# Sample attention: scores of old and appended keys in one hi/lo product, and a value product that runs ahead

## The reference

```
c_kv, k_rope = past latents and rotary keys (512 rows a stream) + 16 new rows
kvb    = c_kv @ w_kv_b                     # per head 64 for keys, 64 for values
k_nope = rmsnorm(kvb[..., :64], k_norm)    # a norm per key row and head
s = (q_nope . k_nope + q_rope . k_rope) * ATTN_SCALE
p = softmax(s);  o = p @ v;  mix = o @ w_o
```

## Time and profile before

| | us |
|---|---|
| median of 3 runs (lowest, highest) | 1978.94 (1974.6, 1982.67) |
| the profiled execution's own time | 1974.86 |
| its span in the profile | 1973.1 |
| TensorE busy (matmul) in the span | 1901.7 |
| VectorE / ScalarE / POOL busy | 1136.4 / 819.5 / 235.3 |
| sample attention, 1487.5 to 1600.0 | 112.5 |

### The profile page before, as it was taken

One profiled execution on the slowest core, in us unless ns is written; L12 is line 12 of the kernel. 1 busy time (PEld: TensorE's weight loads), 2 busy tenths in 40 slices (PEclk: granted clock), 3 DMA queues, 4 the chain that ended last, 5 costly groups with the idle time before them and its releaser, 6 DMA issues.

```text
span 1973.1 us, 28535 instructions
## 1 busy us (share of the span) xinstructions
PE 1901.7 (96%) x10641; PEld 1773.1 (90%) x10641; DVE 1136.4 (58%) x1800; ACT 819.5 (42%) x1428; POOL 235.3 (12%) x338
## 2 busy tenths in 40 slices
PE   9999998999998999999999999989999999999997
PEld 9999998788887999999999999876767779999997
DVE  6555448778779655445855544465654545555444
ACT  5333335555463433334533333355443324333233
POOL 1000110220210000011400002140012222000020
PEclk9999998999999999999999999899999999999999
DMA  5344444455342534444344444430022213444441
GB/s 198 126 128 128 139 148 141 135 176 203 111 181 91 174 125 126 130 136 129 115 140 128 128 135 132 166 101 22 33 66 79 80 51 119 125 124 126 136 138 64
DMA packets 63413, 243.33 MB, mean 123 GB/s; under 512 B 7681, under 2 KB 7761, under 8 KB 62049
## 3 DMA queue, kind: packets, MB, share of 16 engines
q1 hardware_dynamic: 54000, 196.67, 31.7%
q0 software_dynamic: 9328, 45.51, 6.6%
HBM read 230.32 MB, written 11.83 MB: 123 GB/s over the span
## 4 chain that ended last, share of the span: by engine, by line
PE 86%; DVE 7%; ACT 4%; issue 2%; POOL 0%; DMA 0%; SPq 0%; ACTq 0%; DVEq 0%; POOLq 0%
PE bank L1647 23%; PE bank L1649 23%; PE bank L1648 23%; PE bank L2155 2%; PE bank L2112 1%; PE bank L2057 1%; DVE wlo L1054 1%; PE bank L1844 1%; ACT seg L756 1%; PE bank L2059 1%; ACT kn L964 1%; PE bank L2058 1%; PE bank L1654 1%; PE bank L1655 1%; PE bank L1656 1%
## 5 line engine op out<-in xcount | busy, mean ns | idle before, releaser
L1647 PE MATMUL bank<-xh,whi 128*128 128x384 f32 x1960 | 665.7, 340 | 15.1 <-DVE xl L1064 13.2
L1649 PE MATMUL bank<-xh,wlo 128*128 128x384 f32 x1960 | 658.8, 336 | 0.0
L1648 PE MATMUL bank<-xl,whi 128*128 128x384 f32 x1960 | 658.8, 336 | 0.0
L1054 DVE TENSOR_TENSOR wlo<-raw,whi 128x1024 fp32r<-128x1024 f32 (+3 forms) x372 | 463.8, 1248 | 177.8 <-ACT whi L627 169.3
L627 ACT ACTIVATE whi<-raw 128x1024 fp32r<-128x1024 f32 (+2 forms) x369 | 378.9, 1029 | 296.4 <-PE bank L1649 282.4
L1647 PEld LDWEIGHTS bank<-xh,whi 128*128 128x128 f32 x1960 | 371.1, 189 | 25.3 <-issue 14.8
L1648 PEld LDWEIGHTS bank<-xl,whi 128*128 128x128 f32 x1960 | 371.2, 189 | 1.8 <-issue 1.2
L1649 PEld LDWEIGHTS bank<-xh,wlo 128*128 128x128 f32 x1960 | 370.5, 189 | 0.0
L1647 PE MATMUL bank<-ah,whi 128*128 128x384 f32 x704 | 237.2, 337 | 3.5 <-DVE tu L1075 3.3
L1074 DVE TENSOR_TENSOR tg<-bank,rstd 128x384 f32<-128x384 f32 x88 | 49.1, 557 | 331.1 <-PE bank L1649 330.5
L1649 PE MATMUL bank<-ah,wlo 128*128 128x384 f32 x704 | 236.8, 336 | 0.0
(11 more groups left out here) (379 smaller groups left out, 2280.7 us busy)
## 6 DMA issues: line engine op xcount, KB each, us to landing
raw<-in_stream SPq DMA_DIRECT2D x372, 512.0 KB, 3.6
S<-in_ssm POOLq DMA_DIRECT2D x4, 2048.0 KB, 9.1
out_ssm_s<-S POOLq DMA_DIRECT2D x4, 2048.0 KB, 8.0
cTb<-in_cacheT POOLq DMA_DIRECT2D x16, 512.0 KB, 3.8
seg<-acs_rows POOLq DMA_DIRECT2D x12, 512.0 KB, 5.1
lowC<-in_cache POOLq DMA_DIRECT2D x8, 512.0 KB, 3.8
h<-in_x SPq DMA_DIRECT2D x2, 768.0 KB, 5.9
lowA<-in_wkT POOLq DMA_DIRECT2D x4, 384.0 KB, 5.5
```

What stands on the lines that cost most here:

```text
L1054: V.tensor_tensor(wlo[:, r, 0:w], raw[:, r, 0:w], whi[:, r, 0:w].bitcast(F32), ALU.subtract).then_inc(lo_ready, 1)
L1647: M(out, whi[:, r, ws], mh_(k), start=first and k == k0, stop=False)
L1648: M(out, whi[:, r, ws], ml_(k), start=False, stop=False)
L1649: ins = M(out, wlo[:, r, ws], mh_(k), start=False, stop=last and k == k1 - 1)
```

## The change

- The 16 new keys of a stream are appended to its 512 past ones: `cTh`, `cTl` and `cTb` have 528 columns (`KEYS`). The latent query is split too: `QCh` and `QCl`, which live in the slots of `whi` and `wlo`. A unit's scores (`s_scores`) are 12 fp32r matmuls of 264 columns into two banks (`pair[1]`), and 2 for the rotary part into `pair[2]`. For the latter, high, low and high rows of 32 stand on each other (`q_stack`, `k_stack`, 96 rows). The rotary queries are stacked into `xh` and `xl` during the prompt heads.
- Each stream's latent is loaded once more and split once more for that (`keys_split`, on ScalarE and VectorE). From stream 2 on it comes into one buffer `craw`, and the rotary keys of every stream into one buffer `kraw`.
- The key factors are transposed once (`rs_turn`), stored to DRAM (`rs_rows`), and loaded for each unit with every row repeated 16 times (`past_rstd_rows` into `kn`). POOL's copies, the four transposes of a unit and the copy L1007 go.
- The maximum and the exponential go over 528 columns at once. The probabilities are scaled by the reciprocal of their sum before they are transposed, where the output was scaled after.
- The value product is turned: latent rows stationary, the probabilities of both units of a stream (`PTs`, 256 columns) moving, so that the output comes out turned. `s_values(n)` does half c of the 256 features of stream b, `b, c = divmod(n, 2)`; each half is issued two units after its unit. `s_turn`, L1622 and L1608 go; ScalarE copies the result (`s_latent`).
- Since `QCh` and `QCl` use the weight slots, the first three blocks of the output projection are split behind the loop. The reciprocals of `ksq` are taken in parts, streams 0 to 5 in the last prompt heads, 6 and 7 after.

The diff, cut to its core:

```diff
 # POOL
+            pool.wait_ge(rs_ev, 2)
+            pool.dma_start(rs_past(0, 6, 0, 3 * P), rsT[0:6 * MH, :]).then_inc(rs_st, 16)
+            pool.dma_start(rs_past(0, 6, 3 * P, P), rsT2[0:6 * MH, 0:P]).then_inc(rs_st, 16)
             for x in range(0, MH, MH // 4):
                 pool.wait_ge(qk_ps, x + MH // 4)
                 pool.dma_start(wkT[0:QD, x:x + MH // 4], T["wkT"][:, x:x + MH // 4]).then_inc(wkT_ld, 16)
+            def past_keys(b):
...
+                    pool.wait_ge(qc_ps, 8)
+                    pool.wait_ge(past_lo, STREAMS + b)
+                    pool.dma_start(craw, T["cacheT"][b]).then_inc(c_ld[b % 2], 16)
+            def past_rope(b):
...
+                    pool.wait_ge(stack_lo, 2 + b)
...
+                pool.dma_start(kraw[:, 0:PAST], T["krcT"][b]).then_inc(rope_ld, 16)
+                pool.dma_start(kraw[:, PAST:KEYS], kr_spread(b)).then_inc(rope_ld, 16)
+            def past_values(b):
+                pool.wait_ge(po_ps, MH + 2 * max(b - 1, 0))
                 pool.dma_start(cnat[:, b % 2], T["cache"][b]).then_inc(cn_ld[b % 2], 16)
+                pool.dma_start(vnew[0:STEPS, b % 2, :], ckv[STEPS * b:STEPS * b + STEPS, 2, :]).then_inc(cn_ld[b % 2], 16)
+            def past_rstd_rows(u):
+                if u >= 2:
+                    pool.wait_ge(s_added, u - 1)
+                pool.dma_start(kn[:, u % 2, 0:KEYS], rs_spread(u)).then_inc(rk_ld[u % 2], 16)
...
+            for u in range(2, UNITS):
+                b = u // 2 + 1
+                if u % 2 == 0 and b < STREAMS:
+                    past_keys(b)
+                    past_rope(b)
...
+                past_rstd_rows(u)
+                if u % 2 and b < STREAMS:
+                    past_values(b)
 # ScalarE
+            for u in range(UNITS):
+                if u >= 2:
+                    s_latent(u - 2)
+                if u + 1 < UNITS:
+                    s_exp(u + 1)
+                s_turned(u)
+                if u % 2 == 0 and 2 <= u // 2 + 2 < STREAMS:
+                    keys_split(u // 2 + 2)
 # VectorE
+            s_max(0)
+            keys_split(1)
             for u in range(UNITS):
                 dve.wait_ge(s_exp_ready, u + 1)
+                step(V.reciprocal(sm[:, o + 5:o + 6], sm[:, o + 4:o + 5]))
+                V.tensor_scalar(Pb[:, s, 0:KEYS], Pb[:, s, 0:KEYS], sm[:, o + 5:o + 6], None, ALU.mult).then_inc(p_ready, 1)
                 if u + 1 < UNITS:
                     s_max(u + 1)
+                if u % 2 == 0 and 2 <= u // 2 + 2 < STREAMS:
+                    keys_split(u // 2 + 2)
 # TensorE
+            for u in range(UNITS):
+                if u >= 2:
+                    s_values(u - 2)
+                if u + 1 < UNITS:
+                    s_scores(u + 1)
+                pe.wait_ge(p_ready, MH + u + 1)
+                pe.wait_ge(pt_ev, MH + u)
                 for j in range(5):
                     ins = nc.tensor.transpose(bank[6][:, tiles(j)] if j < 4 else bank[0][:, 0:P], Pb[:, u % 2, tiles(j)], ident[:, :])
                 ins.then_inc(pt_ps, 1)
```

More of the change, by code:

```diff
@@ L111, in build @@
         rows = sb("rows", [P, 2, TT])
-        bank = [ctx.enter_context(nc.psum_tensor(f"bank{i}", [P, 512], F32)) for i in range(8)]
+        pair = [ctx.enter_context(nc.psum_tensor(f"pair{i}", [P, 2, 512], F32)) for i in range(4)]
+        bank = [pair[i // 2][:, i % 2, :] for i in range(8)]
         with ExitStack() as ffn:
@@ L327, in build @@
         qc_ps = sem("qc_ps")
+        qc_hi = sem("qc_hi")
         qc_ev = sem("qc_ev")
[L329 to L334, removed]
+        stack_hi = sem("stack_hi")
+        stack_lo = sem("stack_lo")
+        rs_turn_ps = sem("rs_turn_ps")
+        rs_ev = sem("rs_ev")
+        rs_st = sem("rs_st")
+        rk_ld = [sem(f"rk_ld{i}") for i in range(2)]
         s_added = sem("s_added")
@@ L1026, in _ @@
+            act.wait_ge(sc_ps, UNITS)
+            for b in range(AHEAD):
+                hi_split(WO + b)
+            for n in range(UNITS - 2, UNITS):
+                s_latent(n)
             for x in range(MH // 2):
@@ new lines, in _ @@
+            dve.wait_ge(past_std, 2)
+            V.reciprocal(ksq[:, :, 6:8], ksq[:, :, 6:8]).then_inc(past_rstd, 1)
+            keys_split(0)
+            for j in range(8):
+                dve.wait_ge(qc_hi, j + 1)
+                for k in range(2):
+                    ins = V.tensor_tensor(QCl[:, k, :, 2 * j:2 * j + 2, :],
+                                          bank[j % 4][:, tiles(k, 2 * P)].rearrange("p (h b q) -> p b h q", h=2, b=STREAMS),
+                                          QCh[:, k, :, 2 * j:2 * j + 2, :].bitcast(F32), ALU.subtract)
+                ins.then_inc(qc_ev, 1)
@@ new lines, in s_scores, with s_values @@
+                for a in range(2):
+                    ins = M(pair[2][:, a, 0:264], q_stack(b)[0:3 * ROPE, g, :], k_stack(b)[:, 264 * a:264 * a + 264],
+                            start=True, stop=True)
+                ins.then_inc(sc_ps, 1)
+            def s_values(n):
+                b, c = divmod(n, 2)
+                pe.wait_ge(pt_ev, MH + 2 * b + 2)
+                pe.wait_ge(cn_ld[b % 2], 32 * (b // 2 + 1))
+                if b:
+                    pe.wait_ge(s_out_kept, n - 1)
+                for j in range(5):
+                    v = cnat[:, b % 2, j, tiles(c)] if j < 4 else vnew[:, b % 2, tiles(c)]
+                    ins = M(bank[1 if c else 7][:, 0:256], v, PTs[:, b % 2, j, :], start=j == 0, stop=j == 4)
+                ins.then_inc(po_ps, 1)
@@ L2148, in _ @@
                 ins.then_inc(pt_ps, 1)
-                if u + 1 < UNITS:
-                    s_rope(u + 1)
-                pe.wait_ge(pt_ev, MH + u + 1)
-                if u % 2 == 0:
-                    pe.wait_ge(cn_ld[b % 2], 16 * (b // 2 + 1))
-                for j in range(5):
-                    ins = M(bank[7][:, 256:512], PT[:, tiles(j)], cnat[:, b % 2, j, :] if j < 4 else ckv[:, 2, :],
-                            start=j == 0, stop=j == 4)
-                ins.then_inc(po_ps, 1)
-            s_turn(UNITS - 1)
+            s_values(UNITS - 2)
+            s_values(UNITS - 1)
             pe.wait_ge(s_out_kept, 2 * STREAMS)
@@ L2164, in _ @@
                 for k in range(2):
-                    ins = M(o, wv[:, k, VH * x:VH * x + VH], QC[:, k, :, x, :], start=k == 0, stop=k == 1)
+                    ins = M(o, wv[:, k, VH * x:VH * x + VH], OL[:, k, :, x, :], start=k == 0, stop=k == 1)
                 if x % 2:
```

335 lines of the change are left out of this document (183 added, 152 removed).

## The result

| | us |
|---|---|
| after, median of 4 runs (lowest, highest) | 2062.32 (2058.76, 2065.12) |
| before, median of 4 runs of the same comparison | 1976.77 (1968.76, 1982.67) |
| ratio, 95% interval | 1.0435 (1.0392 to 1.0477) |
| span of the profiled execution, whose own time is 2065.12 | 2063.2 |

The change makes the kernel 4.35% slower: 86 us by the medians, 90.1 by the spans (2063.2 less 1973.1). The forecast was 2036 with a range up to 2058, so the time lies 4 us beyond its upper end.

The account below looks back on a forecast made before the run. The prediction took TensorE alone to bound sample attention before the change. It summed 1974.9 + 36 (loop) + 14 (clock) + 7 (ahead of the loop) + 3 (prompt heads) = 2034.9, and said 2036 us, range 2005 to 2058.

Parts of the forecast that it names:

- predicted walk: Sample attention loop: one pair's chain through POOL, load, ScalarE, VectorE and TensorE, 19.5 us in place of 13.2.
- t0: Sample attention loop: end of an odd `s_values`, from which each pair was timed; first at 27.5 us, 23.3 after the last.
- Landing 3.8 us after its issue, it is there at 4.9: Loop: the next stream's latent, issued after `past_values`' two issues, lands 4.9 us into the pair.
- +36: Sample attention loop: 148.5 us against 112.4; bounds +15 if loads landed at once, +42 at 5 us a landing.
- 5 us a landing: Loop: upper bound on the latent's landing time, 6 us more in all, giving +42.
- +14: Loop: TensorE's clock low when the value product starts, 2.35 us lost per pair, some seven bursts; bounds 0 and +50.
- +7 and +3: Ahead of the loop: `wkT` issued later and added copies, +7; reciprocals, rotary splits and copies in the prompt heads, +3.
- The splits moved behind the loop: Output projection's weight splits: lie beside the last two value products (4.4 us); without that cover they would cost 4.
- TensorE stays the bound: Rival for the loop: loads land before the splits ask, a pair falls under 8.9 us; 1960 us, 6%.
- Only the order costs: Rival for the loop: latents there in time, pairs of 16 us, loop 127, clock +6; 2006 us, 9%.
- No change: Rival for the loop: queues overlap better, ScalarE's copy ahead of the exponential, loop 109; 1982 us, 3%.
- stay down throughout: Rival: TensorE's clock down through the whole loop, +50 in place of +14; 2072 us, 5%.

Follow-up runs that it names:

- experiment 1: The changed kernel with POOL issuing the next stream's latent and rotary keys ahead of `past_values` and its `po_ps` wait: 2039.53 us, loop 163.0.
- experiment 3: The changed kernel with ScalarE copying a unit's transposes ahead of the next unit's exponential, POOL's order unchanged: 2038.70 us, loop 164.8.
- experiment 8: The changed kernel with latent and rotary keys still waiting for the value product, but issued ahead of the value rows: 2054.34 us, loop 177.8.
- experiment 5: The changed kernel with unused fp32 matmuls filling TensorE's stops in five pairs: 2052.9 us, loop 174.2.
- experiment 4: The changed kernel with `wkT` and stream 0's latent and rotary keys issued ahead of the `rs_ev` 2 wait and two stores: 2051.99 us.
- experiment 2: experiment 1 with the next unit's key factors' load also issued ahead of `past_values`: 2022.06 us, loop 143.3.
- experiment 6: experiment 2 with ScalarE's order made transposes' copy, keys split, exponential: 1983.45 us, ratio 1.0013, loop 105.9.
- experiment 9: The kernel before, with only the output projection's first three blocks' splits moved behind the loop: 1981.26 us, ratio 0.9988.

## Why the prediction was right in kind, and where it failed

*The bound of the kernel before, and the chain after: right.* Every station of the predicted walk is in the chain, in its order, and all but two last about as long as the rows of before said. The walk has two slips, which nearly cancel: 6.2 + 1.23 + 0.17 + 0.7 is 8.3 and not 8.1 (1 us over five pairs), and the terms behind the last t0 add up to 22.9 and not 23.3. Experiments 1 and 3 show that both causes it named are real, the loads behind `po_ps` and the exponential ahead of the copy.

*The step that failed: "Landing 3.8 us after its issue, it is there at 4.9".* The 3.8 of the earlier trace rows is of latents asked for alone, or with few loads beside them. Here seven loads, 1766 KB together, are issued within some 4 us of one event, and the latent, third of them, lands after 6.0 to 7.0 in the five pairs. The term of the sum is +36, and it is too small by about 17 us: 2.8 for each of five pairs, and 3.1 for the key factors' load that ends the loop (6.66 in the chain, 3.5 taken). The bound of "5 us a landing" came from the same solitary loads, which is why the range was too low. Experiment 8 shows that its place in the burst is the cause: in front of the value rows it lands in 4.2. How the burst shares its time isn't shown. By the Trainium skill, DMA: Bandwidth & Descriptors, Two DMAs through the same engine are not ordered, descriptors within one queue of a DMA engine start in order but are pipelined, and a later one may end first. The trace agrees: the first 512 KB land in 3.5 us and the second in 6.6, and the rotary keys asked for behind the latent land 2.0 us ahead of it. That page's estimate for a load by itself (Anatomy of one DMA), 3.2 us for 512 KB in the prediction, is half of what was measured.

*The clock: right, in part by luck.* +14 was taken. Pairs measure 24.7 us on average, 19.5 + 2.8 for the load leave 2.4, 12 in five pairs; the first units (31.4 us to the first t0 in place of 27.5) and the last (28.8 in place of 23.3, of which 3.1 is the load) add 3.9 and 2.4. So 18 are left beside the loads: 148.5 + 17 + 18 = 183.5, measured 183.7. Counted in the chain, the clock is 14 of them: seven even value products of 4.0 to 4.6 us in place of 2.4 are some 13, and the first scores, at 0.22 us an instruction in place of 0.12, 1.4. The filling of experiment 5 gives back 9 in five pairs. The rest is small: in a pair the gap of 0.28 ahead of POOL's first issue and the 0.2 of the slip. The luck is in the size for one burst: the prediction let the low level last 4.7 us and cost 2.35. But the kernel before still has 1.00 from 1477 to 1478, when that work begins, and 0.85 from 1478 to 1479. Its low level lasts some 3.4 us and costs 1.7, near the 1.8 of a value product here; the sum took 14 of the 16 for seven bursts, and left out the first scores. The prediction's premise, the low level after each long stop, is in the rows above. By the Trainium skill, TensorE: Matmul & The Clock Gate, HAM oscillation, bursts parted by waits pay the half clock each time; the trace agrees, the first eight instructions of the value product take 3.5 to 3.8 us at all seven of these starts, and 1.99 at full clock.

*Ahead of the loop: +7 and +3, measured 15.7 in all.* The same error again: the last part of `wkT` landed in 8.4 and not in 5.5. That 5.5 is a median over loads of two kinds, three asked for in a row (median 6.2) and one alone (3.7). Behind that, the stop cost the query products the clock as well, 8.0 + 1.3 by experiment 4, with 1.8 more between them and the scores than before. The prompt heads' +3 was 4.6.

*The splits moved behind the loop: costed at 0, gave 3.8.* The prediction asked only what they cost where they go, not what they held up where they stood. The chain of before has them (0.85 on ScalarE and 1.57 on VectorE from 1298.78); it was not read there.

The errors by the spans: +21 in the loop, +5.7 ahead of it, +4.2 from the difference between executions less the missed gain, -1.1 behind: 30 us over the 2034.9 of the sum. The median of the runs lies 2.8 below the profiled one, and 2036 was 1.1 above the sum, which leaves the 26 us between 2036 and 2062.

*The rivals.* That TensorE stays the bound fell with its 95 busy us of 182 in the loop. "Only the order costs" put a loop of 127 and a clock of 6 on it, 2006; experiment 2 is that kernel, with a loop of 143 and 2022. "No change" named its condition, ScalarE's copy ahead of the exponential with the loads in time and a loop of 109: experiment 6 has both (and the split ahead of the exponential), 105.9 us, 1983 where this rival said 1982, and a total within 0.2% of before. The clock did not stay down throughout: 0.72 in the loop, and 1.00 in the second half of each burst.

## What to carry to other kernels

A load's landing time belongs to the place where it is issued as much as to its size: before a landing is taken from another stage, count what else the same queue issues in the microseconds before it, and put the load that the chain needs first, ahead of every wait that isn't its own. Fewer cycles on the bounding engine are worth nothing until the order on every other queue has been walked through once round the loop; here the orders on POOL and ScalarE cost 79 us, and with them mended the loop is 8 us shorter than before (104.2 in place of 112.4). When work is moved, read the chain at the place that it leaves too.

## What was not expected of the hardware

- 512 KB land in 3.5 us as the first of seven loads in one queue, and in 6.6 as the third, asked for 1.1 us later; alone or ahead of the others, in 3.8 and 4.2. But the value rows as the fourth, behind 710 KB, take 4.3 (experiment 8), and a later and smaller load can land first. The 264 KB of key factors, rows of 528 values each repeated for 16 partitions, take 7.0 at the end of the burst and 4.8 where the burst is broken into smaller groups (medians of the change and of experiment 2).
- Unused matmuls in a stop shortened the loop by 9.5 us, by keeping the granted clock at 0.90 in place of 0.72 (experiment 5).
- The granted clock can be low or not behind the same stops: behind a stop of 0.85 us the last value product had 1.00 in the kernel before and 0.50 in experiment 9.
- The edits together gave more than alone: 40 and 24 us alone, 79 together with a third order.
